# Attention over sixteen heads in a fused two-block kernel: eight probability buffers in place of six, scores four head pairs ahead in place of three

## The reference, cut to what matters

```
s_c = einsum('bqghd,bngd->bghqn', q_b, k_cmp) + head_bias(dist_c)
p_c = masked_softmax(s_c, mask_c)
o_c = einsum('bghqn,bngd->bqghd', p_c, v_cmp)
...
s_s = einsum('bqghd,bgqkd->bghqk', q_b, k_g) + bias_s
p_s = masked_softmax(s_s, mask_s)
o_s = einsum('bghqk,bgqkd->bqghd', p_s, v_g)
...
s_w = einsum('bqghd,bkgd->bghqk', q_b, k_w) + head_bias(dist_w)
p_w = masked_softmax(s_w, mask_w)
o_w = einsum('bghqk,bkgd->bqghd', p_w, v_w)
return g_b[..., 0:1] * o_c + g_b[..., 1:2] * o_s + g_b[..., 2:3] * o_w
...
h = post_norm(h, mix, ln_g[layer, 1], ln_b[layer, 1])
```

## Time and profile before

| | us |
|---|---|
| median of three runs | 1459.88 |
| the three runs | 1460.07, 1459.88, 1457.74 |
| the profiled execution, its own time | 1457.67 |
| its span in the profile | 1455.9 |
| PE busy in the span | 1436.2 (99%) |
| DVE busy | 1076.6 (74%) |
| ACT busy | 679.0 (47%) |
| POOL busy | 207.2 (14%) |

### The profile page before, as it was taken

The page is one execution under the profiler, slowest core; times in us unless marked ns, Lnnn a source line. Parts: engine busy times, 40 slices in busy tenths (PEclk is TensorE's granted clock), DMA queues, the critical chain, the costliest instruction groups (busy, mean ns, idle before and its releaser), DMA issues.

```text
span 1455.9 us, 20706 instructions
## 1 busy us (share of the span) xinstructions
PE 1436.2 (99%) x7418; PEld 1208.5 (83%) x7418; DVE 1076.6 (74%) x1818; ACT 679.0 (47%) x848; POOL 207.2 (14%) x191
## 2 busy tenths in 40 slices
PE   9999999999999999999999999999999999999997
PEld 7988897888888888889988888887888897788886
DVE  5765757888778887757658887747877877688876
ACT  6346556544444444444435444445443477454342
POOL 1073011200001000300032000201000325510001
PEclk9999999999999999999999999999999999999999
DMA  8754653855656556465577556675566450465561
GB/s 277 232 172 148 197 175 123 295 191 180 211 185 214 176 179 212 171 217 188 170 233 242 187 175 211 220 231 174 173 198 207 151 172 30 141 235 173 183 214 64
DMA packets 198701, 273.94 MB, mean 188 GB/s; under 512 B 9585, under 2 KB 158193, under 8 KB 198386
## 3 DMA queue, kind: packets, MB, share of 16 engines
q1 hardware_dynamic: 194130, 256.10, 53.5%
q0 software_dynamic: 4368, 16.78, 3.3%
q10 hardware_dynamic: 144, 0.26, 0.0%
HBM read 271.80 MB, written 1.31 MB: 188 GB/s over the span
## 4 chain that ended last, share of the span: by engine, by line
PE 89%; DVE 3%; POOL 3%; ACT 2%; issue 1%; DMA 1%; SPq 0%; DVEq 0%; ACTq 0%; POOLq 0%
PE ps L663 25%; PE ps L665 25%; PE ps L664 25%; PE ps L775 3%; PE ps L758 3%; PE ps L769 3%; PE ps L704 1%; ACT whi L1415 1%; POOL wlo L2740 1%; DMA raw<-in_w_in 1%; PE ps L1153 0%; PE ps L1189 0%; PE ps L1254 0%; DVE wlo L1977 0%; DVE big L2564 0%
## 5 line engine op out<-in xcount | busy, mean ns | idle before, releaser
L1977 DVE TENSOR_TENSOR wlo<-raw,whi 128x2048 fp32r<-128x2048 f32 (+1 forms) x221 | 502.4, 2291 | 171.5 <-ACT whi L1415 169.6
L1415 ACT CAST whi<-raw 128x2048 fp32r<-128x2048 f32 (+1 forms) x236 | 447.0, 1894 | 375.6 <-PE ps L665 328.5
L663 PE MATMUL ps<-whi,st_hi 128*128 128x512 f32 x1048 | 410.4, 392 | 0.0
L665 PE MATMUL ps<-whi,st_lo 128*128 128x512 f32 x1048 | 408.0, 389 | 0.0
L664 PE MATMUL ps<-wlo,st_hi 128*128 128x512 f32 x1048 | 407.9, 389 | 0.0
L2391 DVE STREAM_TRANSPOSE hidT<-hidden 32x128 f32<-32x128 f32 x800 | 242.3, 303 | 12.3
L665 PEld LDWEIGHTS ps<-whi,st_lo 128*128 128x128 f32 x1048 | 196.7, 188 | 41.0
L663 PEld LDWEIGHTS ps<-whi,st_hi 128*128 128x128 f32 x1048 | 196.8, 188 | 40.7 <-issue 0.3
L664 PEld LDWEIGHTS ps<-wlo,st_hi 128*128 128x128 f32 x1048 | 196.8, 188 | 40.2
L663 PE MATMUL ps<-whi,hid_hi 128*128 128x512 f32 x400 | 156.2, 390 | 1.3 <-DVE hid_lo L2403 1.3
L665 PE MATMUL ps<-whi,hid_lo 128*128 128x512 f32 x400 | 155.7, 389 | 0.0
(11 more groups left out here) (262 smaller groups left out, 1420.6 us busy)
## 6 DMA issues: line engine op xcount, KB each, us to landing
raw<-in_ffn_w SPq DMA_DIRECT2D x264, 512.0 KB, 4.9
raw<-in_w_gate_up SPq DMA_DIRECT2D x44, 512.0 KB, 4.8
raw<-in_w_in SPq DMA_DIRECT2D x32, 512.0 KB, 5.1
raw<-in_sgu_w_in SPq DMA_DIRECT2D x32, 512.0 KB, 4.7
raw<-in_w_down SPq DMA_DIRECT2D x22, 512.0 KB, 5.0
raw<-in_sgu_w_out SPq DMA_DIRECT2D x16, 512.0 KB, 4.8
raw<-in_kv_w SPq DMA_DIRECT2D x12, 512.0 KB, 4.6
raw<-in_w_proj_attn SPq DMA_DIRECT2D x8, 512.0 KB, 4.7
```

Source lines behind the costliest of these rows:

```text
L663: pe.matmul(o, a[0], b[0], start=start, stop=False)
L665: return pe.matmul(o, a[1], b[0], start=False, stop=stop)
L1415: act.copy(whi[:, s, 0:n], raw[:, s, 0:n]).then_inc(whi_ready, 1)
L1977: dve.tensor_tensor(wlo[:, s, 0:n], raw[:, s, 0:n], whi[:, s, 0:n].bitcast(F32), ALU.subtract).then_inc(wlo_ready, 1)
```

## The change

`prob2` becomes a list of eight buffers of 768 floats. Six lie where they lay, and two are the first 768 floats of the two rows of `gb`; heads 6, 7, 14 and 15 (pairs 3 and 7) use these. The small tiles `rowmax`, `rowsum` and `factor` grow with them. `scores2(4)`, `max2(4)`, `factors2(3)` and `exp2(4)` move out of the loop, ahead of pair 1, and inside the loop every one of these steps is a pair further. `load_norm(4)` moves from the front of the attention to behind POOL's last scaling, where it first waits until pair 7 is transposed. No instruction is added or taken away.

```diff
-        prob2 = carve(11488, 6, 768)
+        prob2 = [carve(11488 + 768 * b, 768) for b in range(6)] + [gb[:, r, 0:768] for r in range(2)]
@@ PE
             scores2(3)
             queries(3, (1,))
+            scores2(4)
             values2(0)
             cmp_scores(1)
...
             for i in range(1, HEADS2 // 2):
                 turn2(i)
-                if i + 3 < HEADS2 // 2:
-                    scores2(i + 3)
+                if i + 4 < HEADS2 // 2:
+                    scores2(i + 4)
@@ ACT
             exp2(3)
+            exp2(4)
             cmp_exp(1)
             for i in range(1, HEADS2 // 2):
                 heads_out(i - 1)
                 if i == 4:
                     cmp_turned(1)
                 turned2(i)
-                if i + 3 < HEADS2 // 2:
-                    exp2(i + 3)
+                if i + 4 < HEADS2 // 2:
+                    exp2(i + 4)
@@ DVE
-                if i >= 3 and 1 in heads:
+                if i >= 4 and 1 in heads:
 
-                    dve.wait_ge(*full(("T2b", i - 3)))
+                    dve.wait_ge(*full(("T2b", i - 4)))
...
             max2(3)
+            max2(4)
+            factors2(3)
             cmp_in_exp(1)
             for i in range(1, HEADS2 // 2):
-                if i + 3 < HEADS2 // 2:
-                    max2(i + 3, (1,))
+                if i + 4 < HEADS2 // 2:
+                    max2(i + 4, (1,))
                 heads_out(i - 1)
                 turned2(i)
+                if i + 4 < HEADS2 // 2:
+                    max2(i + 4, (0,))
                 if i + 3 < HEADS2 // 2:
-                    max2(i + 3, (0,))
-                if i + 2 < HEADS2 // 2:
-                    factors2(i + 2)
+                    factors2(i + 3)
@@ POOL
             layer_norm(("ffn", 3), first["k2"])
-            load_norm(4)
...
                 mm.then_inc(prob_ready, 1)
+            pool.wait_ge(*full(("T2b", 7)))
+            load_norm(4)
             layer_norm("nsa", first["ffn", 4])
```

More of the change, by code:

```diff
@@ L111, in build @@
         top8 = sb("top8", [P, 8])
-        rowmax = sb("rowmax", [P, 6, 4])
+        rowmax = sb("rowmax", [P, 8, 4])
         negmax = sb("negmax", [P, 3, 4])
-        rowsum = sb("rowsum", [P, 6, 4])
-        factor = sb("factor", [P, 6, 4])
+        rowsum = sb("rowsum", [P, 8, 4])
+        factor = sb("factor", [P, 8, 4])
         cmp_stat = sb("cmp_stat", [P, 3, 32])
@@ L1294, in turn2 @@
                     pe.wait_ge(prob_end_ready, h + 1)
-                    pr = prob2[:, h % 6, :]
+                    pr = prob2[h % 8]
                     room(("T2", h))
@@ L1877, in part @@
                 def part(h, x):
-                    b = h % 6
+                    b = h % 8
                     lo = (0, P, S, 2 * S)[x]
                     n = (P, P, S, S)[x]
-                    return act.activation(prob2[:, b, lo:lo + n], prob2[:, b, lo:lo + n], ACT.Exp,
+                    return act.activation(prob2[b][:, lo:lo + n], prob2[b][:, lo:lo + n], ACT.Exp,
                                           bias=rowmax[:, b, x:x + 1], scale=-1.0, accum_out=rowsum[:, b, x:x + 1])
@@ L2555, in max2 @@
             def max2(i, heads=(1, 0)):
-                if i >= 3 and 1 in heads:
-                    dve.wait_ge(*full(("T2b", i - 3)))
+                if i >= 4 and 1 in heads:
+                    dve.wait_ge(*full(("T2b", i - 4)))
                 def part(h, tb, L):
-                    b, n = h % 6, P * (tb + 1)
+                    b, n = h % 8, P * (tb + 1)
                     for br in range(2):
                         lo = S * tb + n * br
-                        mm = dve.tensor_tensor_reduce(prob2[:, b, lo:lo + n], L[:, n * br:n * br + n],
+                        mm = dve.tensor_tensor_reduce(prob2[b][:, lo:lo + n], L[:, n * br:n * br + n],
                                                       view(bias2[:, h, n - 1:n], (-1, n)), -1.0, 3e38, ALU.add, ALU.min,
@@ L2642, in factors2 @@
                     dve.wait_ge(factor_ready, h + 1)
-                    seg = prob2[:, b, 2 * S:3 * S]
+                    seg = prob2[b][:, 2 * S:3 * S]
                     dve.tensor_scalar(seg, seg, factor[:, b, 3:4], None, ALU.mult).then_inc(prob_end_ready, 1)
@@ L2912, in _ @@
                 for x in range(3):
-                    seg = prob2[:, b, (0, P, S)[x]:(P, S, 2 * S)[x]]
+                    seg = prob2[b][:, (0, P, S)[x]:(P, S, 2 * S)[x]]
                     mm = pool.tensor_scalar(seg, seg, factor[:, b, x:x + 1], None, ALU.mult)
                 mm.then_inc(prob_ready, 1)
+            pool.wait_ge(*full(("T2b", 7)))
+            load_norm(4)
             layer_norm("nsa", first["ffn", 4])
```

## The result

The changed kernel took 1461.61 us (median of 19 runs, 1458.75 to 1463.49), the kernel before 1459.9 (median of 19, 1457.45 to 1461.34). The ratio is 1.0015 with a 95% interval of 1.0009 to 1.0022: slower by 1.3 to 3.2 us, about 2.2, which is real and small (the ratio is made over all the runs; the two medians alone differ by 1.7 us). The prediction was 1461.0 and 1.1 us slower.

A forecast was written before the change was run, and what follows sets the result against it. The prediction took PE as the bound, busy 1436.2 of 1455.9 us. Pair 4's 1.45 later, less 0.28 and 0.15, made 1.0 to 1.1; taking 1.1 slower than the 1459.88 median gave 1461.0 us, range 1457.6 to 1463.8.

The forecast's parts named there:

- ACT decides: Attention loop: ACT's early exponentials stand ahead of copies PE waits for; L1325 of pair 4 comes 1.45 us later.
- A: Theory from the follow-up runs, not the prediction: the cost is ACT's order in the attention loop, 1.02 us in the stretch.
- The pause at pair 4: PE at pair 4 waits for ACT at L1320 and again 0.45 at L1325: 2.1 us, where it lost 0.63.
- What comes back: End of the attention loop: 0.28 us of PE's waiting at pair 5 and 0.15 for POOL at pair 7 return.
- The norm's load: Moved behind POOL's last scaling: lands by 1256.2, at latest 1260.2, ahead of its first read; cost nothing.
- The size of the whole: Whole kernel: 1.1 us slower, 0.08%, giving 1461.0 us; 0.82 chance of lying within 0.2%.
- the clock: PE's clock falls at pair 4's 2.1 us pause, adding 1.7 to 3.4 us: 1462.7 to 1464.4; chance 0.08.
- Rival 1: Attention loop: the lead works, ACT's row maximum waits (2.1 us) vanish; 1458.9, at best 1457.6; chance 0.13.
- Rival 2: Attention loop: the lateness cancels within one or two pairs, PE's gap at pair 4 is 0.6; 1459.9; chance 0.11.
- Rival 4: The norm's load lands late, taking over 13.5 us; at 5 us late 1466; chance 0.02.

The follow-up runs named there:

- the three groups: The changed kernel, nothing further altered, timed in three groups of runs against the kernel before: ratios 1.0015, 1.0018 and 1.0010.
- the changed kernel's fifth profile: The changed kernel profiled again, nothing further altered: stretch 55.20 us, PE's clock falling at pair 4; its run's ratio to the kernel before 1.0010.

## Why the prediction was right, step by step

- **ACT decides.** Right, and shown by four runs that change only ACT's place or load at pair 4 or what PE does meanwhile: 51.45, 52.19 and 52.23 us where A says 51.5, 52.3 and 52.2, and L1325 of pair 4 4.8 us later (4.5 to 5 expected) where the same order stands in the old kernel. Less the 0.76 us that lay ahead of the attention, L1325 of pairs 1 to 4 came at 1216.37, 1221.71, 1227.28 and 1233.25; the prediction had 1216.4, 1.4 to 1.5 behind 1220.20 and 1225.78, and 1233.2.
- **The pause at pair 4.** 1.59 + 0.49 of lost time (L1325 follows L1320 by 0.97 instead of 0.48), 2.1 as said.
- **What comes back.** Pair 5's L1325 follows L1320 by 0.49, so its 0.28 is back. POOL ended pair 7 at 1239.37 and took 4.15 us for it in place of 7.83; its 0.15 of waiting is gone. Sum in the trace 1.02, predicted 1.0 to 1.1.
- **The norm's load.** Right: issued at 1249.57 and 1250.20, landed after 4.1 and 5.1 us, so by 1255.3, first read at 1264.2. All thirteen traces, with the load moved or not, have 201.0 to 201.1 us behind the stretch.
- **The size of the whole.** Here the forecast was short: 1.1 against 2.2 (1.3 to 3.2), and only the 1.0 in the attention was derived and found. Of the further 1.1 us a part is the term I gave a chance of 0.08 as a rival, the clock. I took it as one case or none; it is a thing that some executions of the same kernel meet and others don't, 1.6 us each time. It was seen in one of five profiles of the changed kernel, which would make 0.3 us on average. Of its 41 times in the three groups 9 lie over 1462.6 us where no run of the kernel before does; if only executions of the later of the two groups of the last section can get there (58 of the 94 times of the kernel before are in it), that is about one in three, an estimate of 0.6 us. For a share above 0.3 speaks also that whole time less stretch is 1.1, 1.6 and 0.4 us in the changed kernel's three groups and 0.0 to 0.5 in the five kernels without the pause of 1.6 us whose profiles show no fall; against it, each of these is uncertain by 1.3 us. So the clock as a part is shown, its share is an estimate, and the rest is open. That 1461.0 lies only 0.6 us from the measured median is in part luck: neither of these stands in the sum.
- **The rivals.** Rival 1 needed ACT's waits for the row maxima to vanish; they are 0.49, 0.52 and 0.52 us. Rival 2 needed pair 7's exponentials done ahead of 1229.9; they ended at 1231.3 by the same correction. Rival 4 had no sign of it.

**The 0.76 us ahead of the attention.** 0.6 of it arises at one place, long before the change. At 275.7 us the first profile of the changed kernel is 0.06 us behind that of the kernel before; then ACT waits for a weight unit to land, DVE's rest of it and PE's next matmul follow late, and from 283 us on it is 0.67 behind. ACT's rows there, in the kernel before, the changed kernel, and the changed kernel again:

```profile
277.93 1.91 ACT L1415 CAST whi<-raw 128x2048 fp32r<-128x2048 f32 x1 [5.98 <-DMA raw<-in_w_gate_up]
...
278.57 1.91 ACT L1416 CAST whi<-raw 128x2048 fp32r<-128x2048 f32 x1 [6.56 <-DMA raw<-in_w_gate_up]
...
281.28 1.91 ACT L1416 CAST whi<-raw 128x2048 fp32r<-128x2048 f32 x1 [7.02 <-DMA raw<-in_w_gate_up]
```

The step that PE makes there, against the profile before, is 0.6, 1.0, 0.1, 0.7 and 0.2 us in the five profiles of the changed kernel, 0.1 to 0.6 in the six other kernels with its buffers, and 0.3 in the one other profile with the old ones. So one program scatters by 0.9 us at this load alone, and it explains the start of 1205.77. Whether the changed kernel is also later there on average can't be told from so few profiles.

## What to carry to other kernels

A deeper lead moves every engine's share of a step earlier, also on the engine that the others wait for, so look first at what now stands ahead of the instruction that is waited for: here the eight buffers with the orders mended gave 50.45 us against 52.54, but ACT's late exponentials had to stay behind its copies. (Whether six buffers with DVE's order mended would give a part of that was not run.) Where a pipeline drains, the stages that were fed early leave a hole that the slowest engine fills alone. For changes of 0.1% compare two fixed points inside the traces: in four of five profiles the stretch repeated to 0.06 us, where whole times spread over 4.

## What the runs showed of the hardware

**The kernel's times fall into two groups, and its first matmuls tell which.** All 94 times of the kernel before lie at 1457.0 to 1458.3 or at 1459.7 to 1461.5, and none between. Its profile (1457.67) and that of the changed kernel run again (1462.08) are one of each sort. In the first, the four matmuls L830 start at 4.87 us and take 1.98; in the second they start at 4.92 and take 3.78:

```profile
4.92 3.78 PE L830 MATMUL ps<-gb,big 1*128 1x512 f32 x4
8.63 1.22 PE L824 MATMUL ps<-big 128*128 128x128 f32 x4
```

At 275.7 us PE is then 2.3 us late. The thirteen traces fall in the same two sorts: in five, L830 takes 1.98 to 2.14 us and pair 3's scores start at 1202.42 to 1203.18; in eight it takes 3.78 and they start at 1204.68 to 1205.77. The fall of the clock in 8 to 12 us does not make the difference: four of the five traces with the short L830 have it, the fifth (the changed kernel's fifth profile) has not, and its scores start no earlier. The twofold duration of L830 is that of the lower of the two levels, 1.2 GHz, though the row of busy time says 1.00 there (9 matmuls in 4 to 8 us against 18 before). That the level is the cause is read from these durations; no run changed it.

**Where the clock falls in mid-kernel differs from run to run of one program.** It fell behind a stretch of small matmuls without a wait (0.66 in 1214 to 1219 us), behind a pause with PE busy 0.80 of 2.70 us in one profile of five, and in and behind 5 us of standing still. The Trainium skill, "TensorE: Matmul & The Clock Gate", part 1, says that an idle array falls to 1.2 GHz; the 0.50 and 0.51 behind the two pauses agree, while the first fall came with PE busy 3.00 of the 3.00 us before it. So a pause of 1.6 us can cost 1.6 us more than itself, and a kernel can be slower by it in a part of its runs.
